# A fused two-block kernel on one core: the first stage reordered by tiles of tokens

## The reference, cut to what matters

```python
n = rmsnorm(h, g_mix[l])          # h: 256 x 1024
proj = n @ w_in[l]                # many column groups, one of them each:
(b_gate, c_gate, h_conv, q, k_c, v_c, k_s, v_s, k_w, v_w,
 g_br, g_conv, g_attn) = jnp.split(proj, split_pts, axis=-1)
k_cmp = compress(kvh(k_c), ...)   # blocks of 32 tokens, two small layers
v_cmp = compress(kvh(v_c), ...)
o_all = nsa_attention(q, k_cmp, v_cmp, selb(k_s), selb(v_s), winp(k_w), winp(v_w), overlap, n_top)
```

## Time and profile before

| | us |
|---|---|
| median of 3 runs | 746.34 (745.74 to 746.81) |
| the profiled execution | 746.17 |
| its span, first to last instruction | 744.4 |
| TensorE matmul busy | 739.7 (99%) |
| DVE busy | 518.2 (70%) |
| ACT busy | 416.7 (56%) |
| POOL busy | 66.8 (9%) |

### The profile page before, as it was taken

One profiled execution on the slowest core, in us unless ns is written; L12 is line 12 of the kernel. 1 busy time (PEld: TensorE's weight loads), 2 busy tenths in 40 slices (PEclk: granted clock), 3 DMA queues, 4 the chain that ended last, 5 costly groups with the idle time before them and its releaser, 6 DMA issues.

```text
span 744.4 us, 11570 instructions
## 1 busy us (share of the span) xinstructions
PE 739.7 (99%) x4557; PEld 640.6 (86%) x4557; DVE 518.2 (70%) x834; ACT 416.7 (56%) x788; POOL 66.8 (9%) x103
## 2 busy tenths in 40 slices
PE   9999999999999999999999999999999999999998
PEld 8999989877888888888888888887888888888886
DVE  5784777885756678887367757898667777447762
ACT  6575557456464455565356547697646656346640
POOL 7300000000010000530000004400100000000000
PEclk9999999999999999999999999999999999999999
DMA  8998454343455547766656562735355655656611
GB/s 268 286 324 270 87 124 139 114 141 123 133 170 197 179 150 220 199 213 227 187 175 205 170 226 59 254 116 179 109 166 170 195 200 175 221 169 186 210 57 56
DMA packets 99209, 131.26 MB, mean 176 GB/s; under 512 B 5357, under 2 KB 79163, under 8 KB 99156
## 3 DMA queue, kind: packets, MB, share of 16 engines
q1 hardware_dynamic: 96564, 125.58, 52.6%
q0 software_dynamic: 2304, 4.43, 2.8%
q10 hardware_dynamic: 288, 0.52, 0.2%
HBM read 128.68 MB, written 1.84 MB: 175 GB/s over the span
## 4 chain that ended last, share of the span: by engine, by line
PE 97%; DVE 2%; ACT 1%; issue 0%; POOL 0%; POOLq 0%
PE B L1628 39%; PE B L1594 22%; PE B L1599 11%; PE B L1583 11%; PE B L1809 2%; PE B L1856 2%; PE B L1819 2%; PE B L1641 1%; PE B L1692 1%; DVE LO L1004 1%; PE B L1635 1%; PE B L1812 1%; PE B L1836 1%; PE B L1737 1%; PE B L1795 0%; PE B L1736 0%
## 5 line engine op out<-in xcount | busy, mean ns | idle before, releaser
L1004 DVE TENSOR_TENSOR LO<-RAW,HI 128x1024 fp32r<-128x1024 f32 x236 | 282.6, 1236 | 100.8 <-ACT HI L540 100.2
L1628 PE MATMUL B<-HI,AA 128*128 128x512 f32 (+1 forms) x960 | 286.7, 376 | 0.3 <-DVE AA L1010 0.2
L540 ACT ACTIVATE HI<-RAW 128x1024 fp32r<-128x1024 f32 (+1 forms) x240 | 237.1, 1039 | 61.8 <-PE B L1628 58.1
L1628 PEld LDWEIGHTS B<-HI,AA 128*128 128x128 f32 x960 | 175.7, 188 | 33.8 <-issue 1.4
L1594 PE MATMUL B<-AA,HI 128*128 128x512 f32 x704 | 179.2, 393 | 0.0
L1628 PE MATMUL B<-LO,AA 128*128 128x512 f32 (+1 forms) x480 | 178.6, 372 | 0.0
L1594 PEld LDWEIGHTS B<-AA,HI 128*128 128x128 f32 x704 | 126.7, 189 | 23.0 <-issue 0.7
L1628 PEld LDWEIGHTS B<-LO,AA 128*128 128x128 f32 x480 | 90.5, 189 | 14.7
L1599 PEld LDWEIGHTS B<-AA,LO 128*128 128x128 f32 x704 | 96.6, 190 | 7.1
L1599 PE MATMUL B<-AA,LO 128*128 128x256 f32 x704 | 98.8, 282 | 0.0
L1583 PE MATMUL B<-AA,HI 128*128 128x256 f32 x448 | 83.3, 287 | 0.0
(11 more groups left out here) (313 smaller groups left out, 634.2 us busy)
## 6 DMA issues: line engine op xcount, KB each, us to landing
RAW<-in_w_in SPq DMA_DIRECT2D x29, 1024.0 KB, 5.6
RAW<-in_w_gate SPq DMA_DIRECT2D x22, 1024.0 KB, 5.3
RAW<-in_w_up SPq DMA_DIRECT2D x22, 1024.0 KB, 5.4
RAW<-in_w_down SPq DMA_DIRECT2D x22, 1024.0 KB, 5.0
RAW<-in_w_in SPq DMA_DIRECT2D x10, 512.0 KB, 6.5
RAW<-in_w_attn_out SPq DMA_DIRECT2D x4, 1024.0 KB, 5.0
RAW<-in_w_o SPq DMA_DIRECT2D x4, 1024.0 KB, 4.9
RAW<-in_w_out SPq DMA_DIRECT2D x4, 1024.0 KB, 5.0
```

The lines of the kernel that those rows point to most:

```text
L540: e.activation(pieces(HI, NSPL, i, k), pieces(RAW, NRAW, i, k), ACT.Copy).then_inc(split_hi, 1)
L1004: e.tensor_tensor(pieces(LO, NSPL, i, k), pieces(RAW, NRAW, i, k), pieces(HI, NSPL, i, k), ALU.subtract).then_inc(split_lo, 1)
L1628: x = e.matmul(dst, a, w[:, t, c0:c0 + n], start=(first and t == 0 and k == 0), stop=(last and t == nk - 1 and k == 2))
```

## The change

Seven edits:

1. **Loads.** ACT's queue starts half 0 of both tiles of x, the sync queue half 1 of both. The gain row is started by GpSimd, right after its first memset.
2. **Norm by tiles.** Tile 0 has its own mean and its own root; ACT sums half 0 and DVE half 1 of tile 0; ACT sums both halves of tile 1. The later roots are renumbered. GpSimd runs both roots of the norm ahead of its twelve small row loads (`VR`).
3. **Scaling.** DVE scales all four pieces; ACT's two scalings go. DVE also makes the high copy of the first piece.
4. **Order of units.** The selected values become unit 0, and units 0 to 11 become 1 to 12. From unit 13 on nothing moves.
5. **TensorE's start.** 9 idle products, gain row, 6 idle products; then the values by quarters (one tile, one half, one kind of product, four matmuls), between the four turns and the relative bias product; then the selected keys, all eight row chunks of one kind after the other.
6. **End of the first stage.** The values no longer stand between the last queries and the attention. One piece of `fill()` (window keys 0) is taken ahead of the first scores, so step 0 takes one piece after them. ACT's loop is as before.
7. **ACT and GpSimd.** ACT copies the values of tile 0, then does `hi(2)`, then copies the values of tile 1. GpSimd's bias transfer waits for the queries instead of the values.

```diff
-            for h in range(2):
-                e.dma_start(X[:, 0, halves(h)], A["x"][0, 0:128, halves(h)]).then_inc(x_in[h], 16)
-                if h == 0:
-                    e.dma_start(GAIN[0:128:64, :], ...).then_inc(row_in, 16)
+            for t in range(2):
+                e.dma_start(X[:, t, halves(1)], A["x"][0, 128 * t:128 * t + 128, halves(1)]).then_inc(x_in[2 * t + 1], 16)
...
+            e.wait_ge(squares0_sb, 2)
+            mean(0).then_inc(mean_sb, 1)
             e.wait_ge(gain_pe, 1)
...
+            own.step(e.tensor_tensor(TOK[:, 0, halves(0)], X[:, 0, halves(0)], B[2][:, :], ALU.mult))
+            e.wait_ge(root_sb, 1)
+            own.wait()
+            e.tensor_scalar(TOK[:, 0, halves(0)], TOK[:, 0, halves(0)], ST[:, 6:7], None, ALU.mult).then_inc(scaled_sb, 1)
+            normed(0, 1)
+            e.wait_ge(squares_sb, 4)
+            mean(1).then_inc(mean_sb, 1)
+            e.wait_ge(turn_pe, 1)
+            e.tensor_copy(AH[:, 0:4, 0:128], ...).then_inc(turn_hi, 1)
+            turned(0, B[5], 0, 0)
             lo(0, 0)
+            e.wait_ge(root_sb, 2)
+            for h in range(2):
+                e.wait_ge(x_in[2 + h], 16)
+                normed(1, h)
+            turned(1, B[6], 4, 0)
             lo(0, 1)
+            turned(2, B[5], 0, 1)
+            turned(3, B[6], 4, 1)
             lo(1)
+            lo(2)
...
+            values(0, 0)
+            hi(2)
+            values(0, 1)
...
-            idle(14)
+            idle(9)
...
+            first_turn(0)
+            first_turn(1)
+            quarter(0, 0, AH, hi, True)
+            quarter(0, 0, AL, hi)
+            quarter(0, 1, AH, hi)
+            quarter(0, 0, AH, lo)
+            first_turn(2)
+            e.matmul(B[4][0:4, 0:ROW], REL[:, :], OH[:, :], ...).then_inc(rel_pe, 1)
+            first_turn(3)
+            quarter(1, 0, AH, hi, True)
+            quarter(1, 0, AH, lo)
+            quarter(0, 1, AL, hi)
+            quarter(1, 1, AH, hi)
+            quarter(0, 1, AH, lo, last=True).then_inc(vals_pe, 1)
+            quarter(1, 1, AH, lo)
+            for h in range(2):
+                x = quarter(1, h, AL, hi, last=True)
+            x.then_inc(vals_pe, 1)
...
             queries(3, 1)
-            for t in range(2):
-                values(U_VALS, 0, t)
...
+            filler = fill()
+            next(filler)
             e.wait_ge(q_sb, 8)
...
                 if i < NSTEP:
                     scores(i)
-                for _ in range(FILL_AT[i]):
+                for _ in range(FILL_AT[i] - (i == 0)):
                     next(filler)
```

More of the change, by code:

```diff
@@ L401, in _ @@
             e.wait_ge(setup, HALF)
-            e.memset(REL[32:33, :], NEG).then_inc(far_set, 1)
+            e.memset(REL[32:33, :], NEG).then_inc(setup, 1)
+            e.wait_ge(setup, FAR)
+            root(1, ST[:, 6:7], ST[:, 4:5], 1)
+            e.wait_ge(root_sb, 1)
+            root(2, ST[:, 7:8], ST[:, 5:6], 1)
             e.dma_start(VR[0:12, :], A["conv_w"][0].rearrange("k (c p) -> (k c) p", p=128)).then_inc(rows_in, 16)
@@ L456, in _ @@
             e.wait_ge(rel_sb, 1)
-            e.wait_ge(vals_sb, 2)
+            e.wait_ge(q_sb, 8)
             e.dma_start(bias_rows.rearrange("h r n -> h (r n)").rearrange("h (r n) -> h r n", n=ROW),
@@ L472, in _ @@
             gain(1, A["attn_norm_g_2"][0, :])
-            root(2, ST[:, 6:8], ST[:, 4:6])
+            root(3, ST[:, 6:8], ST[:, 4:6])
             e.wait_ge(gain_in[0], 16)
@@ L527, in _ @@
             own = Own(e, act_step)
-            for h in range(2):
-                e.dma_start(X[:, 1, halves(h)], A["x"][0, 128:256, halves(h)]).then_inc(x_in[2 + h], 16)
+            for t in range(2):
+                e.dma_start(X[:, t, halves(0)], A["x"][0, 128 * t:128 * t + 128, halves(0)]).then_inc(x_in[2 * t], 16)
             def hi(i, k=None):
@@ L545, in turned, with squares @@
                              ACT.Copy).then_inc(turn_hi, 1)
-            def squares(col, src, scrap, h):
+            def squares(col, src, scrap, h, done=squares_sb, by=1):
                 e.activation(scrap[:, halves(h)], src[:, halves(h)], ACT.Square, scale=1.0 / 32,
[L549 to L553, removed]
-            hi(0, 0)
[L555 to L559, removed]
-                    for t in range(2):
-                        turned(t, B[5 + t], 0, t)
+                             accum_out=ST[:, col + h:col + h + 1]).then_inc(done, by)
+            e.wait_ge(x_in[0], 16)
+            squares(0, X[:, 0, :], QK[:, 0, :], 0, squares0_sb)
+            e.wait_ge(x_in[2], 16)
+            squares(2, X[:, 1, :], QK[:, 1, :], 0, squares_sb, 3)
+            e.wait_ge(x_in[3], 16)
+            squares(2, X[:, 1, :], QK[:, 1, :], 1)
+            hi(0, 0)
+            e.wait_ge(turn_hi, 1)
+            turned(1, B[6], 4, 0)
             hi(0, 1)
-            for t in range(2):
-                turned(2 + t, B[5 + t], 4, t)
+            turned(2, B[5], 0, 1)
+            turned(3, B[6], 4, 1)
             hi(1)
@@ L1047, in _, with mean, normed @@
-            lo(0, 0)
-            for t in range(2):
-                turned(t, B[5 + t], 0, t)
+            def mean(t):
+                return e.scalar_tensor_tensor(ST[:, 4 + t:5 + t], ST[:, 2 * t:2 * t + 1], EPS, ST[:, 2 * t + 1:2 * t + 2],
+                                              ALU.add, ALU.add)
+            def normed(t, h):
+                e.scalar_tensor_tensor(TOK[:, t, halves(h)], X[:, t, halves(h)], ST[:, 6 + t:7 + t], B[2 + h][:, :], ALU.mult,
+                                       ALU.mult).then_inc(scaled_sb, 1)
@@ L1050, in _ @@
+            for h in range(2):
+                e.wait_ge(x_in[2 + h], 16)
+                normed(1, h)
+            turned(1, B[6], 4, 0)
             lo(0, 1)
-            for t in range(2):
-                turned(2 + t, B[5 + t], 4, t)
+            turned(2, B[5], 0, 1)
+            turned(3, B[6], 4, 1)
             lo(1)
+            lo(2)
             e.wait_ge(rows_pe, 1)
             e.tensor_copy(VT[:, 0:51], B[5][:, 0:51]).then_inc(rows_sb, 1)
-            lo(2)
+            lo(3)
             def block_sums(kv, src, c):
@@ L1649, in _, with first_turn @@
             x.then_inc(gain_pe, 1)
[L1650 to L1655, removed]
-            e.wait_ge(setup, IDENT)
[L1658 to L1662, removed]
+            idle(6)
+            e.wait_ge(setup, IDENT)
+            def first_turn(n):
+                e.wait_ge(scaled_sb, n + 1)
+                turn(n, TOK[:, n // 2, halves(n % 2)], 5 + n % 2)
             def keys(i, br, c):
@@ L1670, in values @@
                 moving(i, 0, 256, B[t][:, 0:256], 0, t, t == 0).then_inc(vals_pe, 1)
-            hi, lo = view(HI, U_KEYS), view(LO, U_KEYS)
[L1674 to L1678, removed]
-                    if k == 0:
[L1680 to L1695, removed]
@@ new lines, in _, with quarter @@
+            hi, lo = view(HI, U_VALS), view(LO, U_VALS)
+            def quarter(t, h, a, w, first=False, last=False):
+                d = slice(t * 128, t * 128 + 128)
+                for c in range(4 * h, 4 * h + 4):
+                    x = e.matmul(B[t][:, 0:256], a[:, c, d], w[:, c, :], start=(first and c == 0), stop=(last and c == 7))
+                return x
+            first_turn(0)
+            first_turn(1)
+            take(0, vals_sb, 1)
+            e.wait_ge(split_hi, 1)
+            e.wait_ge(turn_hi, 1)
@@ new lines, in _ @@
+            quarter(0, 0, AH, hi, True)
+            e.wait_ge(turn_lo, 1)
+            quarter(0, 0, AL, hi)
+            e.wait_ge(split_hi, 2)
+            e.wait_ge(turn_hi, 2)
+            quarter(0, 1, AH, hi)
+            unit_ready(U_VALS, 0)
+            quarter(0, 0, AH, lo)
+            first_turn(2)
+            e.wait_ge(rel_in, 32)
+            e.wait_ge(setup, FAR)
+            take(4, rel_sb, 1)
+            e.matmul(B[4][0:4, 0:ROW], REL[:, :], OH[:, :], start=True, stop=True).then_inc(rel_pe, 1)
@@ new lines, in _ @@
+            x.then_inc(vals_pe, 1)
+            hi, lo = view(HI, U_KEYS), view(LO, U_KEYS)
+            e.wait_ge(split_hi, 2 * U_KEYS + 2)
+            for k, (w, a) in enumerate(((hi, AH), (hi, AL), (lo, AH))):
+                if k == 2:
+                    unit_ready(U_KEYS, 1)
+                for c in range(2):
+                    if k == 0:
+                        take(c, keys_sb, c + 1)
+                    for t in range(8):
+                        x = e.matmul(B[c][:, 0:S], w[:, t, 128 * c:128 * c + 128], a[:, t, :], start=(k == 0 and t == 0),
+                                     stop=(k == 2 and t == 7))
+                    if k == 2:
+                        x.then_inc(keys_pe, 1)
```

121 lines of the change are left out of this document (55 added, 66 removed).

## The result

| | before | changed |
|---|---|---|
| median of 8 runs | 746.31 us | 748.52 us |
| lowest to highest | 745.74 to 747.32 | 747.34 to 750.36 |
| span of the profiled execution | 744.4 | 746.9 |

The ratio is 1.0034, 95% interval 1.0025 to 1.0042: slower by 2.2 us by the medians. The forecast was 747.1, within 744.9 to 748.4; the time lies just above the range.

A forecast was written before the change was run, and what follows sets the result against it. TensorE's stream was taken to bound the kernel; a start of -1.2 us and a seam wait of +1.95 gave +0.75, a median of 747.1 us, counted as no change, within 744.9 to 748.4.

The forecast's parts named there:

- The frame: TensorE's stream from 15.13 us on: it is the limit, so time moves only by an earlier start or a new hole.
- the seam: Window values after the first scores: TensorE waits +1.95 us for ACT's copy of keys 0, bounds 1.4 to 2.1.
- the start: First units of the stream: 1.8 us earlier less 0.6 of added wait, sum -1.2 us, bounds -2.2 to -0.3.
- the wait before the keys' ninth matmul: Keys for bank B[1]: TensorE waits 0.5 to 0.6 us for ACT's copy of the values of tile 1.
- the wait for `q_sb`: Ahead of the first scores: covered by keys 0, since the copy came 0.4 us after the queries and keys take 2.88.
- when the gain row is spread: Start of the kernel: row issued at 1.05, landed at 5.3, DVE released at 6.8 instead of 7.81, 1.0 us earlier.
- rival C: TensorE's start: the clock steps up only after gain passes and six idle products; sum +2.55, 748.9 us; chance 0.15.
- DVE's chain: From DVE's release at 6.8 us through its pieces and the last quarters: unit 0 leaves TensorE at 17.9, 1.8 earlier.
- the earlier bias transfer: GpSimd's bias transfer starts 6 us earlier, at no cost: nobody waits for it before the second block.

The follow-up runs named there:

- e3: Changed kernel with 14 idle products ahead of the gain row instead of 9, the row as late as before: 747.70 us, ratio 1.0021.
- e4: Kernel before with only the seam's edit, window keys 0 taken ahead of the first scores on TensorE: 747.91 us, ratio 1.0023.
- e1: Changed kernel with ACT's high copies of unit 15 and copy of window keys 0 moved ahead of the first exponents: 747.89 us, ratio 1.0024.
- e7: Changed kernel with the seam's order as before, no piece ahead and two after the first scores: 747.79 us, ratio 1.0027.
- e2: Changed kernel with the gain row started by the sync queue instead of GpSimd: 746.55 us, ratio 1.0011.
- e11: e1 with GpSimd's start of the bias transfer moved behind the last scores: 755.19 us, ratio 1.0121.
- e8: e7 with the first scores waiting for four query copies instead of eight: 748.08 us, ratio 1.0034.
- e9: e8 with the gain row started by the sync queue: 744.86 us, ratio 0.9988 against the kernel before.
- e10: e9 with ACT copying the values of tile 1 ahead of the two high copies of unit 2: 746.08 us, ratio 0.9995.

## Why the prediction was wrong

**The frame held.** TensorE's stream is rigid; time moved only by the start and by one hole, and the two sum to the 2.5 us of the span. Against the forecast, the seam is right within 0.1 and the start is off by 1.9: forecast -1.2, measured +0.7. Three pieces make that up: DVE was released at 7.69 instead of 6.8 (0.9 late: the row 1.2 late, the gain passes 0.3 shorter than the 1.4 that I gave them); from there to the keys' first matmul it took 12.26 us instead of 11.1, and 11.08 in e3 with the full clock (1.2 for the clock); the wait before the keys' ninth matmul was 0.2 shorter than forecast.

**The seam was right**: forecast +1.95, measured +1.85, at the matmul, by the copy and in the order named; e4 shows it by itself, e1 that ACT's order is the cause. Only the moment was misread: near 75 to 77 us was named, and the wait stands at 80.8 to 82.6, because the values' 5.76 us moved to the start and everything up to the seam moved later with them. What I called covered there (the wait for `q_sb` by keys 0) was covered; without keys 0 it is a step of 0.75 instead of 0.2 (e7).

**The step that failed is the first term, when the gain row is spread.** I had issue at 1.05 and landing at 5.25 to 5.75, from GpSimd's first two transfers before, and took 5.3. It was issued at 1.34 and landed at 6.47: 5.13 from issue, longer than either row. Five small loads behind them on that queue took 4.7 to 5.0, so about 5 would have been the prudent reading; and the issue instruction began 0.33 after the memset. The Trainium skill (DMA: Bandwidth & Descriptors, section Latency and other measured facts) gives about 1 us to the first byte on GpSimd's path; no row here shows a first byte, and the landing came 5.13 us after the issue. Against a row in time (e3 against e2) the late one costs 1.4 us in the profiles, 1.15 in the medians.

**The second failed term is the clock, which the sum put at nothing.** I gave rival C 0.15, saying that the gap was a few tenths. With the late row it was 1.38 us. In the profiled execution the clock had risen before the gain passes (these took the full-clock 1.13) and fell behind them; that cost 1.2 us in the profiles (changed kernel against e3), 0.8 in the medians. C's own form, a clock that rises only behind the gain passes and the idle products, happened too. It stands in the profile of e11, which has the changed kernel's start:

```profile
6.31 2.08 PE L1658 MATMUL B<-TMP,ones 1*128 1x512 f32 x4 [1.04 <-DMA TMP<-in_g_mix]
8.32 2.93 PE L1651 MATMUL B<-ones 128*128 128x128 f32 x12
```

All executions, by time and mean granted clock (us; number of runs in brackets):

| | clock 0.999 to 1.000, shorter | clock 0.997 or 0.998 | clock 0.999 to 1.000, longer |
|---|---|---|---|
| changed kernel | 747.34, 747.39 (2) | 747.93 to 748.81 (4) | 750.07, 750.36 (2) |
| e1 | 746.97 (1) | 747.55 to 748.60 (7) | 749.49 (1) |
| e7 | 746.29 to 746.77 (4) | 747.24 to 748.94 (4) | 749.14 to 750.01 (3) |
| e8 | 746.54, 746.84 (2) | 747.53 to 748.13 (3) | 749.32 to 749.95 (3) |
| e2, row in time | 746.24 to 746.67 (8) | none | 747.51 to 749.01 (3) |
| e9, row in time | 744.53 to 745.17 (8) | none | 746.54 to 747.07 (3) |
| e10, row in time | 744.12 to 744.82 (5) | none | 746.08 to 747.42 (6) |
| e3, late row, 14 idle products | 747.39 to 748.16 (11) | none | none |

The middle column is the clock that falls behind the pause: with the row in time no run is in it. The last column is C's form by what its one profile shows, e10's 746.11 (the mean does not count the slow time ahead of the first rise); for the other runs of that column there is no trace. C's sum, 748.9, gives 750.1 with the row 1.2 later than I had it (an estimate); the changed kernel's two runs took 750.1 and 750.4. The Trainium skill (TensorE: Matmul & The Clock Gate, Part 1: The HAM clock gate) says that the clock is throttled by default and that activity releases it. The runs agree as far as they go: the last column is filled only where 9 idle products stand ahead of the row, and it is empty in e3 with 14.

**DVE's chain was right** given its two inputs: from DVE's release to the keys' first matmul the forecast had 11.1 us (6.8 to 17.9), e3 took 11.08 and e2 11.30. Its terms as written add up to 17.74, not 17.9; the runs do not tell the two apart. The added wait for the values of tile 1 was forecast at 0.5 to 0.6 and was 0.40, a step of 0.52 less the usual 0.12.

**One claim was wrong without effect here**: that the earlier bias transfer matters to nobody before the second block. Weight units issued while it runs land late (29.5 us after issue in the changed kernel). TensorE's wait at 120.7 in e1 comes from such a unit (e11 takes it away); the wait at 119.6 in e8 ends in one by its chain. In the changed kernel there is no such wait; it showed in e1 when the wait at the seam was gone. Why the transfer takes 34.9 us in e9 and 36.7 to 36.8 in e1, e8 and the changed kernel is open.

## What to carry to other kernels

A load moved to another queue is costed from the slowest landing of that queue at that time, and the idle products in front of it are sized for that; here a pause there was paid twice in most runs, once as the wait and once in TensorE's clock. Runs are sorted by their granted clock before medians are compared. A piece of filler taken ahead on TensorE must be taken ahead on the engine that frees its bank as well, and then the next slack in the loop must be looked up: removing the first wait brought 0.6 of 1.85 us. A long transfer belongs where the weights have a lead: here, moved to where TensorE takes a unit every 5.8 us, it cost 7.6 us.

## What the runs showed of the hardware

The bias transfer is 768 KB from four partitions and takes 34 to 38 us. The weight units issued meanwhile land late and close behind one another: before the change those issued at 80.5, 93.3 and 106.2 us landed at 111.0, 113.8 and 116.5, where the one issued ahead of the transfer, at 70.9, took 5.3 us. In the first stage the first of them lands just after the transfer. The ACT rows that start on that unit, and the transfer's own rows, in e9:

```profile
72.48 1.13 POOL L460 DMA_DIRECT2D bias_rows<-OH  x1 [43.93 <-ACT QT L601]
...
109.38 2.00 ACT L542 ACTIVATE HI<-RAW 128x1024 fp32r<-128x1024 f32 x2 [1.99 <-DMA RAW<-in_w_in]
```

It landed 34.9 us after issue, at 107.4, and ACT went on at 109.4. Before the change it was 109.0 and 111.0, in e8 110.1 and 112.0, in e1 111.2 and 113.2: about 2 us each time. It is not so everywhere: in e11, where the transfer landed at 265.7, a unit issued at 229.9 landed at 260.8. Why they are late no run shows.

The granted clock can fall while TensorE is at work: in the changed kernel it stood from 5.1 to 6.5, worked without a break from then on, and the clock fell at 8.3. The length of the pause does not decide it: in e7 and e8, with pauses of 1.26 and 1.02 us at the same place, the profiled executions kept the clock, and in e1, with 1.20, it fell. In these four profiles another thing goes with it: the 18 idle passes ahead of the pause took 4.07 and 4.11 us in the changed kernel and e1, where the clock rose during them, and 4.21 in e7 and e8, where it rose in the pause. It fell later only in the first two. Four profiles make no rule.

The first rise itself comes at different times in the same start. By the pace of the passes it was there at about 5.7 us in e9 and 10.3 in e10, and at 14.1 in e11.
